# Four output units of an attention stage, moved from steps 6, 7, 9 and 10 to steps 5, 7, 8 and 9

## The chip, the cores and the metric

The kernel runs on one core of one Trainium2 chip. The time is the device time of one execution in microseconds (us). A core has TensorE (PE; PEld is its weight load), VectorE (DVE), ScalarE (ACT), GpSimd (POOL) and SyncE (SP), which issues the weight transfers. The engines run programs of their own and wait for each other through semaphores.

## The reference, cut to what matters

The whole computes two layers with recurrent mixers, then one transformer layer with sliding-window attention and an MLP, for 256 tokens and a width of 1024. The change touches the attention:

```python
def swa_mixer(h, w_qkv, sinks, w_o):
    qkv = h @ w_qkv
    q, k, v = jnp.split(qkv, [SWA_HEADS * HD, (SWA_HEADS + KV) * HD], axis=-1)
    ...
    s = jnp.einsum('bnqkgd,bnskd->bnkgqs', q, kb).astype(jnp.float32) * (HD ** -0.5)
    logits = jnp.where(mask[None, :, None, None], s + bias, NEG)
    m = jnp.maximum(jnp.max(logits, axis=-1, keepdims=True), sink)
    p = jnp.exp(logits - m)
    probs = p / (jnp.sum(p, axis=-1, keepdims=True) + jnp.exp(sink - m))
    o = jnp.einsum('bnkgqs,bnskd->bnqkgd', probs.astype(vb.dtype), vb)
    return o.reshape(B_, T, SWA_HEADS * HD) @ w_o
```

There are 16 heads of 64 columns, 256 tokens in two tiles of 128, and 1024 output columns. The residual, a norm and the MLP follow.

## The kernel before

Matrix products with weights are made of fp32r parts: each operand is split into a high half (a copy rounded to fp32r) and a low half (what is left), and three matmuls are summed (L504 high by high, L505 and L506 the two mixed ones). Weights come in units of 128x1024 in a ring of six slots: SP loads a unit (L436), ACT writes its high half whi (L1132), POOL its low half wlo (L478, L479, raising lo_done), and TensorE raises split_used when it has read one.

**The attention** works on rows r = 0 to 7, each of them two heads. For each row four engines take turns:
- TensorE makes the scores (L1001, L1002) into a pair of PSUM banks. All scores use the same pair, so those of row t wait until VectorE has freed it of row t - 1 (pair_free, a semaphore raised by VectorE's queue at L1620).
- VectorE adds the distance term, takes the minimum (four pieces, L2211), and then makes the reciprocal of the sums of the row before (L2193).
- ScalarE takes the exponentials (four, L1548). GpSimd multiplies by the reciprocals (L463, att_scale).
- TensorE transposes the probabilities (six, L1017), VectorE copies them to pt (L2224, att_pt), and TensorE multiplies them with v (twelve matmuls, L1028 to L1030, att_o).
- ScalarE writes the high half ya_hi of the result (L1555), VectorE the low half ya_lo (L2230, att_ready, one for each row).

The order is written out by hand, in a loop over steps t on each engine. In step t TensorE makes the scores of row t, then a unit of other work if there is one (a q unit for t below 5, an output unit later), then the transposes of row t - 2, then the products with v of row t - 3. ScalarE in step t takes the exponentials of row t and then the high half of row t - 3, which its queue therefore never reaches before the exponentials are done. VectorE in step t reads the scores of row t, then copies the probabilities of row t - 2, then makes the low half of row t - 4; from t = 7 on the low half of row t - 4 comes first.

**The output projection** has two column halves c (512 columns each, one pair of banks each) and four quarters q (two rows each) of the inner dimension. o_unit(c, q) is a whole unit: both tiles of tokens, 12 matmuls of 128x512. It waits for att_ready at 2q + 2, the low halves of rows 2q and 2q + 1, and for q = 0 also for its bank pair (the pair of c = 1 is that of the scores). The units with q of 2 and 3 are cut in halves of one token tile each and follow the loop, as eight half units. In the texts O00, O01, O10 and O11 stand for o_unit(0, 0), (0, 1), (1, 0) and (1, 1); S, T and V with a row's number stand for the scores, the transposes and the products with v of that row.

The lines that place the whole units in the loop on TensorE:

```python
                if t < 5:
                    q_unit((t + 3) // 2, (t + 3) % 2)
                if t in (6, 7, 9, 10):
                    o_unit(t // 9, {6: 0, 7: 1, 9: 0, 10: 1}[t])
                if 2 <= t < 10:
                    r = t - 2
                    pe.wait_ge(att_scale, r + 1)
```

Of the kernel before, what the change touches and what calls it, by code (L numbers as in the profile page):

```python
# [152 lines left out]
def build(nc, a, units, x_turned, p_turned, table, consts, out):  # L153
    with ExitStack() as ctx:
# [247 lines left out]
        def pair_of(name, i):  # L402

            return DB[PAIR[(name, i)]]
# [5 lines left out]
        def score_block(t, head, b):  # L410

            return lg[:, t % 3, LG * head + (P + 1) * b:LG * head + (P + 1) * b + P]
# [80 lines left out]
        def _(pe):  # L493
            at = {"unit": 0}

            def group_start(name, i):

                if BEFORE[(name, i)] > 0:
                    pe.wait_ge(pair_free[PAIR[(name, i)]], BEFORE[(name, i)])
# [30 lines left out]
            def token_unit(name, i, q, xh, xl, start, stop):  # L530

                wh, wl = unit_ready()
                bank = pair_of(name, i)
                for kk in range(SPLK):
                    k = q * SPLK + kk
                    for t in range(NT):
                        tok = slice(t * P, (t + 1) * P)
                        last = three(bank[t][:, :], (xh[:, k, tok], xl[:, k, tok]), (wh[:, kk, :], wl[:, kk, :]),
                                     start=start and kk == 0, stop=stop and kk == SPLK - 1)
                return last  # L540
# [421 lines left out]
            def q_unit(quarter, half):  # L962

                if quarter == 0:
                    bank = pair_of("q_first", 0)[0]
                else:
                    bank = pair_of("q_rest", 0)[(quarter - 1) % 2]
                if half == 0 and quarter < 2:
                    group_start("q_rest" if quarter else "q_first", 0)
                if (quarter, half) == (3, 0):  # L970
                    pe.wait_ge(att_in, 4)
                wide_unit(half, bank, x_hi, x_lo).then_inc(split_used, 1)

            def o_unit(c, q):

                if q == 0:
                    group_start("o_att", c)
                pe.wait_ge(att_ready, 2 * q + 2)
                token_unit("o_att", c, q, ya_hi, ya_lo, q == 0, q == 3).then_inc(split_used, 1)
# [13 lines left out]
            for t in range(11):  # L993
                if t < 8:
                    if t % 2 == 0:
                        pe.wait_ge(att_in, 3 + t // 2)
                    group_start("score", t)
                    bank = pair_of("score", t)
                    for j in range(2):
                        part = slice(j * AD, (j + 1) * AD)  # L1000
                        pe.matmul(bank[j][:, 0:T], qa[part, t, P:T], ka[part, t // 4, :], start=True, stop=True)  # L1001
                        last = pe.matmul(bank[j][:, T:T + P], qa[part, t, 0:P], ka[part, t // 4, 0:P], start=True, stop=True)  # L1002
                    last.then_inc(turned, 1)

                if t < 5:
                    q_unit((t + 3) // 2, (t + 3) % 2)
                if t in (6, 7, 9, 10):
                    o_unit(t // 9, {6: 0, 7: 1, 9: 0, 10: 1}[t])
                if 2 <= t < 10:
                    r = t - 2  # L1010
                    pe.wait_ge(att_scale, r + 1)
                    if r > 0:
                        pe.wait_ge(att_pt, r)
                    for j in range(6):
                        b = high_banks[:, j * P:(j + 1) * P]
                        head, block_ = (j // 2, j % 2) if j < 4 else (j - 4, 2)
                        last = pe.transpose(b, score_block(r, head, block_), ident)  # L1017
                    last.then_inc(att_t, 1)
                if t >= 3:
                    r = t - 3  # L1020
                    pe.wait_ge(att_pt, r + 1)
                    if r - 1 > 0:
                        pe.wait_ge(att_ready, r - 1)
                    v = slice((r // 4) * AD, (r // 4 + 1) * AD)
                    for j in range(2):
                        part = slice(j * AD, (j + 1) * AD)
                        probs = pt[:, r % 2, :]
                        pe.matmul(SB[r % 2][part, 0:P], va[:, 0, v], probs[:, (4 + j) * P:(5 + j) * P], start=True, stop=True)  # L1028
                        pe.matmul(SB[r % 2][part, P:T], va[:, 0, v], probs[:, 2 * j * P:(2 * j + 1) * P], start=True, stop=False)
                        last = pe.matmul(SB[r % 2][part, P:T], va[:, 1, v], probs[:, (2 * j + 1) * P:(2 * j + 2) * P], start=False, stop=True)  # L1030
                    last.then_inc(att_o, 1)
            first = at["unit"]
            at["unit"] += 4
            for t, c, q in ((0, 0, 2), (1, 0, 2), (0, 0, 3), (1, 0, 3), (0, 1, 2), (0, 1, 3), (1, 1, 2), (1, 1, 3)):
# [1429 lines left out]
```

## Time and profile before

| | us |
|---|---|
| median of 3 runs | 918.6 |
| lowest and highest | 918.38 and 918.79 |
| the profiled execution | 918.62 |
| its span in the profile | 916.8 |
| TensorE busy in it | 895.3 |
| POOL, ACT, DVE busy | 674.4, 505.9, 476.2 |

The span is the part of the execution that the profile sees. A row of a timeline gives the start in us from the start of the span, the duration, the engine, the line, the operation, what it writes and reads, shapes, a count where equal ones were merged, and in brackets how long the engine was idle before and what ended it. Matmuls overlap, so a row's end lies behind the start of the next. In the merged rows the duration is that of the whole group. The steps that the change touches lie between 693 and 720 us.

### The profile page before, as it was taken

Reading aid. Unit: us, or ns where it says so; the run is one execution under the profiler, and the core shown is the slowest. Engines: PE = TensorE matmul, PEld = TensorE weight load, DVE = VectorE, ACT = ScalarE, POOL = GpSimd, SP = SyncE. Lnnn points to the kernel's source line nnn. Section 1 sums busy time; section 2 is a strip of 40 time slices with the busy share of each in tenths; the row PEclk is TensorE's granted clock in tenths of the full one; section 3 lists DMA queues with packets and bytes.
Section 4 is the critical chain, followed back from the end, with each engine's and each line's share of the span. In section 5 each row is a group of like instructions: output and inputs, shape, how many; then the busy total and the mean of one; then the engine's idle time right before and its main releaser. Section 6 shows DMA issues by size and latency. Waiting matters only on the chain.

```text
span 916.8 us, 19055 instructions
## 1 busy us (share of the span) xinstructions
PE 895.3 (98%) x7540; PEld 828.6 (90%) x7540; DVE 476.2 (52%) x987; ACT 505.9 (55%) x712; POOL 674.4 (74%) x484
## 2 busy tenths in 40 slices
PE   6999899999999999999999999999999999999997
PEld 6999899998998889999999999888997899998886
DVE  4368865488452533767768777545556442220004
ACT  5775343753336556565677656565566355554431
POOL 5986566566665888967776777769796579889882
PEclk9999999999999999999999999999999999999999
DMA  8663343344443665635444454456552247556631
GB/s 317 203 224 127 127 139 119 120 131 139 140 138 124 209 204 164 207 117 166 157 137 128 153 164 159 138 184 201 179 185 92 93 159 226 190 186 204 205 118 46
DMA packets 41113, 147.14 MB, mean 160 GB/s; under 512 B 4544, under 2 KB 4672, under 8 KB 41024
## 3 DMA queue, kind: packets, MB, share of 16 engines
q1 hardware_dynamic: 39584, 141.76, 47.8%
q10 hardware_dynamic: 1440, 4.16, 1.3%
q8 instruction: 60, 0.98, 0.4%
q14 instruction: 29, 0.24, 0.1%
HBM read 144.86 MB, written 1.05 MB: 159 GB/s over the span
## 4 chain that ended last, share of the span: by engine, by line
PE 89%; DVE 5%; POOL 2%; issue 2%; ACT 2%; DMA 0%; DVEq 0%; ACTq 0%; POOLq 0%
PE dense L504 25%; PE dense L506 24%; PE dense L505 24%; PE bank L872 2%; POOL wlo L479 1%; PE dense L560 1%; POOL wlo L478 1%; PE bank L702 1%; PE bank L703 1%; PE bank L904 1%; PE bank L858 1%; PE bank L1017 1%; PE bank L504 0%; PE bank L506 0%; PE bank L505 0%
## 5 line engine op out<-in xcount | busy, mean ns | idle before, releaser
L479 POOL TENSOR_TENSOR wlo<-raw,whi 128x512 fp32r<-128x512 f32 (+1 forms) x261 | 412.0, 1585 | 25.6 <-ACT whi L1132 25.4
L1132 ACT ACTIVATE whi<-raw 128x1024 fp32r<-128x1024 f32 (+1 forms) x264 | 275.3, 1056 | 226.4 <-PE dense L506 195.8
L478 POOL TENSOR_TENSOR wlo<-raw,whi 128x512 fp32r<-128x512 f32 x197 | 256.4, 1301 | 186.6 <-ACT whi L1132 186.6
L504 PE MATMUL dense<-x_hi,whi 128*128 128x256 f32 x1232 | 353.8, 287 | 8.2 <-DVE wlo L1637 7.3
L505 PE MATMUL dense<-x_lo,whi 128*128 128x256 f32 x1232 | 345.7, 281 | 0.0
L506 PE MATMUL dense<-x_hi,wlo 128*128 128x256 f32 x1232 | 345.7, 281 | 0.0
L504 PEld LDWEIGHTS dense<-x_hi,whi 128*128 128x128 f32 x1232 | 233.9, 190 | 12.1 <-DVE x_lo L1626 7.2
L505 PEld LDWEIGHTS dense<-x_lo,whi 128*128 128x128 f32 x1232 | 235.0, 191 | 0.7 <-issue 0.2
L506 PEld LDWEIGHTS dense<-x_hi,wlo 128*128 128x128 f32 x1232 | 234.5, 190 | 0.0
L504 PE MATMUL dense<-whi,ya_hi 128*128 128x512 f32 x192 | 77.5, 403 | 1.0 <-issue 0.8
L506 PE MATMUL dense<-whi,ya_lo 128*128 128x512 f32 x192 | 75.1, 391 | 0.0
L505 PE MATMUL dense<-wlo,ya_hi 128*128 128x512 f32 x192 | 75.0, 390 | 0.0
L1706 DVE SCALAR_TENSOR_TENSOR cv<-dense,columns,cv 128x255 f32<-128x255 f32 (+2 forms) x72 | 34.7, 481 | 25.8 <-ACT cv L1210 23.2
L504 PEld LDWEIGHTS dense<-whi,ya_hi 128*128 128x128 f32 x192 | 36.1, 188 | 9.0 <-issue 1.7
L506 PEld LDWEIGHTS dense<-whi,ya_lo 128*128 128x128 f32 x192 | 36.1, 188 | 7.8
L505 PEld LDWEIGHTS dense<-wlo,ya_hi 128*128 128x128 f32 x192 | 36.2, 188 | 7.0 <-issue 0.2
L1121 ACT ACT_TABLE_LOAD x32 | 41.1, 1283 | 1.4 <-PEq L2445 0.7
L505 PE MATMUL dense<-wlo,x_hi 128*128 128x256 f32 (+1 forms) x144 | 40.2, 279 | 0.0
L506 PE MATMUL dense<-whi,x_lo 128*128 128x256 f32 (+1 forms) x144 | 40.2, 279 | 0.0
L504 PE MATMUL dense<-whi,x_hi 128*128 128x256 f32 (+1 forms) x144 | 40.1, 278 | 0.0
L2315 DVE TENSOR_TENSOR xtok<-xtok,dense 128x512 f32<-128x512 f32 x2 | 1.4, 686 | 73.6 <-PE dense L506 73.6
L504 PE MATMUL dense<-whi,yb_hi 128*128 128x512 f32 x96 | 37.6, 392 | 0.3 <-POOL wlo L479 0.3
(341 smaller groups left out, 1402.9 us busy)
## 6 DMA issues: line engine op xcount, KB each, us to landing
raw<-weight_units_dram SPq DMA_DIRECT2D x263, 512.0 KB, 3.6
xtok<-in_x_dram SPq DMA_DIRECT2D x1, 1024.0 KB, 7.9
gb<-in_ln_g_dram ACTq DMA_DIRECT2D x2, 512.0 KB, 4.7
gb<-in_ln_b_dram ACTq DMA_DIRECT2D x2, 512.0 KB, 7.0
out_dram<-zt SPq DMA_DIRECT2D x3, 256.0 KB, 2.0
qT<-x_turned_dram SPq DMA_DIRECT2D x2, 256.0 KB, 4.4
raw<-weight_units_dram SPq DMA_DIRECT2D x2, 256.0 KB, 4.9
qT<-x_turned_dram SPq DMA_DIRECT2D x1, 512.0 KB, 7.1
```

Source lines behind the costliest of these rows:

```text
L478: pool.tensor_tensor(wlo[:, slot, 0:half], unit_slot(u)[:, 0:half], whi[:, slot, 0:half].bitcast(F32), ALU.subtract)
L479: pool.tensor_tensor(wlo[:, slot, first:2 * half], unit_slot(u)[:, first:2 * half], whi[:, slot, first:2 * half].bitcast(F32), ALU.subtrac ...
L504: pe.matmul(out_, lh, rh, start=start, stop=False, skip_group_check=True)
L505: pe.matmul(out_, lh, rl_, start=False, stop=False, skip_group_check=True)
L506: return pe.matmul(out_, ll, rh, start=False, stop=stop, skip_group_check=True)
L560: last = pe.transpose(bank[:, j * P:(j + 1) * P], xtok[:, t, k * P:(k + 1) * P], ident)
L702: return pe.matmul(block(SB[2 * g + across], pair, side), block(LT[:, g, :], h, b), block(XN[:, g, :], h, b), start=True, stop=True)
L703: return pe.matmul(SB[2 * g + side][64 * b:64 * b + 64, pair * 32:(pair + 1) * 32], block(EL[:, g, :], 2 * pair + b, side, 256), even_odd( ...
L872: last = pe.matmul(SB[0][rows, u * P:u * P + 96], tokens_of(hk, p % 2, u // 2, u % 2)[:, rows], six, start=True, stop=True)
L1121: act.preload_act_table_set(name)
L1132: act.activation(whi[:, u % NSPL, first:], unit_slot(u)[:, first:], ACT.Copy).then_inc(hi_done, 1)
L1706: link(vec.scalar_tensor_tensor(o, bank[:, i * T:(i + 1) * T - back], colA[:, w:w + 1], o, ALU.mult, ALU.add), conv_done if back == 3 else ...
```

## The change

The first whole unit goes from step 6, between scores and transposes, to the end of step 5, behind the products with v of row 2. The second stays in step 7. The third and the fourth go from steps 9 and 10 to steps 8 and 9, at the same place within the step.

```diff
                 if t < 5:
                     q_unit((t + 3) // 2, (t + 3) % 2)
-                if t in (6, 7, 9, 10):
-                    o_unit(t // 9, {6: 0, 7: 1, 9: 0, 10: 1}[t])
+                if t in (7, 8, 9):
+                    o_unit(t // 8, t % 2)
                 if 2 <= t < 10:
                     r = t - 2
                     pe.wait_ge(att_scale, r + 1)
...
                     last.then_inc(att_o, 1)
+                if t == 5:
+                    o_unit(0, 0)
```

The instructions and their waits stay the same; only TensorE's order differs. The order on TensorE where step 5 passes into step 6, before: the end of V2 (bank01), the scores S6 (dense10, dense11), the beginning of O00 (dense00).

```order
L1028 MATMUL bank01<-pt,va 64x128
L1029 MATMUL bank01<-pt,va 64x128
L1030 MATMUL bank01<-pt,va 64x128
L1001 MATMUL dense10<-ka,qa 128x256 [waits pair_free1,att_in]
L1002 MATMUL dense10<-ka,qa 128x128
L1001 MATMUL dense11<-ka,qa 128x256
L1002 MATMUL dense11<-ka,qa 128x128
L504 MATMUL dense00<-whi,ya_hi 128x512 [waits lo_done,att_ready,pair_free0]
```

And after, at the end of O00, whose twelve matmuls now stand right behind V2: its last rows, S6, and the transposes T4.

```order
L504 MATMUL dense01<-whi,ya_hi 128x512
L505 MATMUL dense01<-wlo,ya_hi 128x512
L506 MATMUL dense01<-whi,ya_lo 128x512
L1001 MATMUL dense10<-ka,qa 128x256 [waits pair_free1,att_in]
L1002 MATMUL dense10<-ka,qa 128x128
L1001 MATMUL dense11<-ka,qa 128x256
L1002 MATMUL dense11<-ka,qa 128x128
L1017 MATMUL bank23<-con,lg 128x128 [waits att_pt,att_scale]
```

The scores of step 6 have moved behind the unit, which keeps its wait for att_ready.

The order on TensorE where step 9 passes into step 10, before: the last matmuls of O11 and the beginning of V7.

```order
L504 MATMUL dense11<-whi,ya_hi 128x512
L505 MATMUL dense11<-wlo,ya_hi 128x512
L506 MATMUL dense11<-whi,ya_lo 128x512
L1028 MATMUL bank01<-pt,va 64x128 [waits att_ready,att_pt]
L1029 MATMUL bank01<-pt,va 64x128
L1030 MATMUL bank01<-pt,va 64x128
```

After: the transposes T7, V6 and V7 in a row.

```order
L1017 MATMUL bank23<-con,lg 128x128 [waits att_pt,att_scale]
L1017 MATMUL bank23<-con,lg 128x128 x5
L1028 MATMUL bank01<-pt,va 64x128 [waits att_ready,att_pt]
L1029 MATMUL bank01<-pt,va 64x128
L1030 MATMUL bank01<-pt,va 64x128
L1028 MATMUL bank01<-pt,va 64x128
L1029 MATMUL bank01<-pt,va 64x128
L1030 MATMUL bank01<-pt,va 64x128
L1028 MATMUL bank01<-pt,va 64x128 [waits att_ready,att_pt]
```

O11 has moved ahead of T7, so between V6 and V7 no unit is left.

## Rows read from the trace of the kernel before

**Rows 1.** The page, part 1: engine, busy us, share of the span, instructions.

```profile
PE 895.3 (98%) x7540; PEld 828.6 (90%) x7540; DVE 476.2 (52%) x987; ACT 505.9 (55%) x712; POOL 674.4 (74%) x484
```

**Rows 2.** List of TensorE's waits, whole span: total us, times, longest.

```profile
PE dense L504 <- DVE wlo L1637: 7.3, 1, 7.3
...
PE dense L504 <- issue: 0.8, 1, 0.8
```

**Rows 3.** Timeline of TensorE, 670 us, then steps 5 to 7.

```profile
670.25 0.71 PE L1001 MATMUL dense<-ka,qa 64*128 64x256 f32 x4
...
671.11 0.38 PE L504 MATMUL dense<-x_hi,whi 128*128 128x256 f32 x1
...
695.26 0.43 PE L1028 MATMUL bank<-pt,va 128*64 128x128 f32 x2
...
697.12 0.71 PE L1001 MATMUL dense<-ka,qa 64*128 64x256 f32 x4 [0.72 <-DVEq L1620]
...
698.86 0.47 PE L504 MATMUL dense<-whi,ya_hi 128*128 128x512 f32 x1 [0.81 <-issue]
...
701.71 0.82 PE L1017 MATMUL bank<-con,lg 128*128 128x128 f32 x6
702.46 0.43 PE L1028 MATMUL bank<-pt,va 128*64 128x128 f32 x2
...
703.53 0.71 PE L1001 MATMUL dense<-ka,qa 64*128 64x256 f32 x4
```

**Rows 4.** Timeline of TensorE, steps 7 to 10.

```profile
704.67 0.50 PE L504 MATMUL dense<-whi,ya_hi 128*128 128x512 f32 x1 [0.20 <-DVE ya_lo L2230]
...
707.53 0.82 PE L1017 MATMUL bank<-con,lg 128*128 128x128 f32 x6
708.27 0.43 PE L1028 MATMUL bank<-pt,va 128*64 128x128 f32 x2
...
709.54 0.85 PE L1017 MATMUL bank<-con,lg 128*128 128x128 f32 x6
...
719.02 0.43 PE L1028 MATMUL bank<-pt,va 128*64 128x128 f32 x2
...
720.10 0.51 PE L504 MATMUL dense<-whi,ya_hi 128*128 128x512 f32 x1
```

**Rows 5.** Timeline of VectorE, steps 5 and 6.

```profile
696.83 0.08 DVE L2211 DVE_READ_ACCUMULATOR2_ANT st_att<- 128x1 f32 x1
...
697.34 0.96 DVE L2224 COPY pt<-bank 128x768 f32<-128x768 f32 x1
698.33 0.42 DVE L2230 TENSOR_TENSOR ya_lo<-bank,ya_hi 128x256 fp32r<-128x256 f32 x1
698.79 0.48 DVE L2211 CUSTOM_DVE_ANT_0 lg<-con,dense,lg 128x256 f32<-128x256 f32 x1
...
700.51 0.08 DVE L2211 DVE_READ_ACCUMULATOR2_ANT st_att<- 128x1 f32 x1
```

**Rows 6.** Timeline of ScalarE, step 6.

```profile
700.66 0.49 ACT L1548 ACTIVATE lg<-lg,st_att 128x257 f32<-128x257 f32 x1
...
702.75 0.19 ACT L1548 ACTIVATION_READ_ACCUMULATOR lg<-lg,st_att 128x1 f32 x1
703.70 0.39 ACT L1555 ACTIVATE ya_hi<-bank 128x256 fp32r<-128x256 f32 x1 [0.77 <-PE bank L1030]
```

**Rows 7.** Timeline of GpSimd: scaling of row 7.

```profile
710.72 1.61 POOL L463 TENSOR_TENSOR lg<-lg,rsum 128x512 f32<-128x512 f32 x2 [2.19 <-DVE rsum L2193]
```

**Rows 8.** TensorE at the start; windows: us, busy (instructions), PEclk (granted clock), DMA, GB/s.

```profile
7.62 0.42 PE L505 MATMUL dense<-x_lo,whi 128*128 128x256 f32 x1
...
13.35 0.29 PE L505 MATMUL dense<-x_lo,whi 128*128 128x256 f32 x1
...
910.00:914.00 4.00, 0.82 (x7) 0.62 (x6) 2.85 (x8) 1.13 (x3) 1.45 (x2) 1.00 0.00 0
914.00:915.00 1.00, 0.00 (x0) 0.00 (x0) 0.00 (x0) 0.00 (x0) 0.00 (x0) 0.72 0.45 172
```

## The prediction

> **What bounds the kernel now.** I read the page's first part, then the list of waits, then the timelines of the attention stage engine by engine. TensorE is busy for 895.3 of 916.8 us [rows 1], so a change of order can move the time only where TensorE stands still. The list of its waits has eight lines for the whole span; the longest, 7.3 us, is the start of the kernel, and one of 0.8 us is the wait ahead of the first output unit, which the change moves [rows 2]. The list names no wait of TensorE from 705 us to its last matmul, so what is lost in the attention stage is handed on to the end whole, with nothing behind it that takes it up. Of the matmuls nothing is added or removed, so the question is one sum: how long TensorE waits in steps 5 to 10 before, and how long after.
>
> The timeline before [rows 3, 4], in starts. The products with v of row 2 (V2, step 5) start at 695.26. Such a group holds the queue for 1.07 us (702.46 to 703.53), so TensorE could go on at 696.33. The scores of step 6 (S6) start at 697.12: **0.79 us** of wait, for the bank pair, which VectorE frees after it has read the scores of step 5 (last piece 696.83 to 696.91, 0.21 us before S6 starts) [rows 3, 5]. S6 takes 0.86 us (670.25 to 671.11, a group of scores that nothing held up), which gives 697.98; unit O00 (column half 0, quarter 0) starts at 698.86: **0.88 us**. Scores S7 start at 703.53, so could end the slot at 704.39; unit O01 starts at 704.67: **0.28 us**. The products V4 end their slot at 709.34 and the transposes T6 start at 709.54: **0.20 us**. Together TensorE waits 2.15 us. From T6 on, the rows join without a hole up to the first half unit at 720.10.
>
> What O00 waits for: it needs att_ready at 2, which is the low half of row 1, a subtraction on VectorE at 698.33 of 0.42 us. It ends at 698.75, and O00 starts 0.11 us later [rows 3, 5]. The row's releaser reads "issue", not VectorE, which leaves a doubt; see rival B. VectorE comes to that subtraction after the scores of step 5 and the copy of the probabilities (697.34, 0.96 us). None of these waits for anything that the change moves, so 698.75 stays.
>
> **The change part by part.** 48 matmuls of 128x512 (four units of 12) change places. A unit is 2.86 us in the queue wherever it stands (704.67 to 707.53), the transposes 0.75 (701.71 to 702.46) [rows 3, 4]. No DMA is issued from TensorE's queue. I now lay out the changed order with these durations.
>
> Step 5. O00 stands right behind V2, ahead of S6. TensorE is free at 696.33, the operand comes at 698.75, so O00 starts at 698.86 as before: a wait of **2.53 us**. S6, which filled part of this before, now stands behind the waiting unit and starts at 701.71 instead of 697.12, 4.6 us later. That is the point of the whole sum, since S6 is what three other engines live on.
>
> Step 6. T4 at 702.57, V3 at 703.32, free at 704.39. VectorE reads S6 when its last matmul ends, 0.94 us from its start, so from 702.75 instead of 698.79; the four pieces take 1.80 us (698.79 to 700.59) [rows 5] and end at 704.55. S7 needs the pair freed, 0.21 us later: 704.76, a wait of **0.37 us** where there was none.
>
> Step 7. S7 to 705.62. O01 needs att_ready at 4, the low half of row 3. Its high half is written by ScalarE, and in ScalarE's order that stands behind the four exponentials of step 6. These took from 700.66 to 702.94 [rows 6] and now start behind VectorE's pieces, at 704.61, and end at 706.89. The high half (0.39 us) ends at 707.31, VectorE's subtraction (0.42 us) runs 707.41 to 707.83, O01 starts at 707.90: a wait of **2.28 us** instead of 0.28. Before, this high half waited for V3 alone (703.70, after ScalarE had stood idle for 0.77 us) [rows 6], since the exponentials were long done.
>
> Steps 7 to 10. T5 at 710.76, V4 711.51, O10 712.58 (its pair is free once VectorE has read S7, 707.87 to 709.67), T6 715.44, V5 716.19, O11 717.26, T7 720.12, V6 720.87, free at 721.94. The wait ahead of T6 is gone (0.20 us), because O10 stands over the copy that it waited for. At the end the reverse happens: no unit stands between V6 and V7 any more. V7 needs the copy of T7's transposes: T7's last matmul ends 0.84 us from its start, 720.96, the copy runs 721.05 to 722.01, and V7 starts at 722.13: a wait of **0.19 us**. The first half unit follows 1.08 us later (719.02 to 720.10) [rows 4], at 723.21 instead of 720.10.
>
> The sum: waits 2.53 + 0.37 + 2.28 + 0.19 = 5.37 against 2.15 us, +3.22; by the starts, 723.21 - 720.10 = +3.11, since the slots differ by a few hundredths. I take **+3.1 us**. The profiled execution took 918.62 us, the median is 918.6, so both lead to 921.7.
>
> What I cost at nothing, and its cover. GpSimd scales row 5 from about 705.0 to 706.6 (1.61 us) [rows 7], 4 us before T5 needs it; row 6 and row 7 likewise end 3 us and more ahead. The split of the seventh weight unit of the projection follows the scaling of row 7, which ends about 715.5; its first reader is the fifth half unit, at 723.21 plus four times 1.43 (half of 2.86), about 729, 13 us later. The low half of row 7 ends 1.0 us after V7 as before and is read 2.8 us after the first half unit. Nothing there comes near.
>
> **The clock.** Over 910 to 914 us the granted clock is 1.00 although the last matmul ends at 910.82; in the next microsecond it is 0.72 [rows 8]. So 3.2 us of idle did not take the 2.4 GHz level away in this trace, and the two new holes are 2.5 and 2.3 us. At the start of the kernel, after 7.3 us of idle [rows 2], matmuls of 128x256 ran at 0.42 us each, and from 13.35 at 0.29 [rows 8], the 1.2 GHz and the 2.4 GHz level. The Trainium skill (TensorE: Matmul & The Clock Gate, "HAM oscillation — how this bites in real kernels") speaks against this change in general: long pauses between groups of matmuls let the chip halve the array's clock, and the work after each pause then starts slow. By that rule the sum would be rival C's, by the rows here it is the +3.1 above.
>
> **The rivals.**
> A, the forecast: both waits as laid out, 921.7 us. Its own range: without the two small waits (0.37 and 0.19) +2.5, less the 0.4 us spread of the runs, 920.7; with 0.1 us more at each of the eight handovers, 922.5.
> B, not slower: O00 does not wait for the low half of row 1. The row at 698.86 names "issue" as its releaser, while that at 704.67 names VectorE; if the 0.88 us belong to S6 itself or the sequencer, O00 starts at 696.33 in its new place. Then S6 is at 699.2, VectorE ends it at 702.1, S7 waits 0.37 us (702.24), exponentials end at 704.4, and O01 starts at 705.4; with the same steps behind it the first half unit comes at 720.7, +0.6: 919.2 us. It decides from the point at which O00 starts before about 697.6, which would bring the sum under 1.84 us. Against it: the semaphore's raise and the start are 0.11 us apart. Even then nothing is gained, since S6's delay alone eats the 0.88 us.
> C, slower still: one hole brings the 1.2 GHz level. At the start the low level held from 7.3 to 13.3 us, for 6 us of matmuls [rows 2, 8], half of it lost: at most +3.0 us for one hole, 924.7; for both 927.7. Against it: the clock row at the end.
> D, faster: all waits of steps 5 to 10 vanish, -2.15 us at most, 916.5. It needs the operand of O00 2.5 us earlier, for which nothing in VectorE's order moves.
> That the change does not take place is excluded, as the order of the built kernel shows it.
>
> **How the numbers follow.** A 0.82, B 0.08, C 0.07, D 0.03. A measurement of this kernel can tell about 0.2%, 1.84 us, from no change. Slower by more is A but for its lower edge and C: 0.87; within: B and that edge, 0.10; faster: 0.03. The range is A's, opened upward to most of one hole of C: 920.7 to 924.4.
>
> **What the profile after would show.** O00's first matmul at 698.9 with 2.4 us idle ahead, ending what was S6's place; S6 at 701.7; ScalarE's first exponential of step 6 near 704.6; O01 near 707.9 with over 2 us idle ahead and VectorE's ya_lo as releaser; a small hole ahead of V7; no hole ahead of T6; the first half unit near 723.2; the granted clock 1.00 throughout; every stage behind shifted by 3.1 us. The prediction is wrong if O00 starts at 696.4 (B), if units after a hole take over 4 us (C), or if a hole of over 0.5 us opens or closes anywhere behind 724 us.

## The result and the profile after

| | us |
|---|---|
| before, median of 6 runs | 918.69 (918.38 to 918.97) |
| after, median of 6 runs | 924.25 (921.95 to 925.72) |
| ratio, with its 95% interval | 1.0059 (1.0048 to 1.0069) |
| the profiled execution after, and its span | 924.71 and 922.8 |

The changed kernel is slower by 5.6 us. The range on record holds the time by 0.15 us; the forecast point, 921.7, was 2.5 us too low, so little more than half of the loss was foreseen. The runs after also spread over 3.8 us, those before over 0.6 us. Two lines of the list of waits answer to the one shown in [rows 2] (total in us, times, longest):

```profile
PE dense L504 <- issue: 2.5, 1, 2.5
PE dense L504 <- DVE ya_lo L2232: 2.3, 1, 2.3
```

The hole ahead of O00 is 2.5 us and that ahead of O01 2.3 us, as laid out. From O01's start to the end of the span the list names no further wait of TensorE. The page's first line against [rows 1]:

```profile
PE 897.8 (97%) x7540; PEld 829.6 (90%) x7540; DVE 476.8 (52%) x987; ACT 505.8 (55%) x712; POOL 673.9 (73%) x484
```

TensorE is busy 2.5 us longer, although its matmuls are the same 7540. So holes alone are not the whole loss. The timeline of TensorE, against [rows 3, 4]:

```profile
695.03 0.43 PE L1028 MATMUL bank<-pt,va 128*64 128x128 f32 x2
...
698.63 0.53 PE L504 MATMUL dense<-whi,ya_hi 128*128 128x512 f32 x1 [2.46 <-issue]
...
700.24 0.63 PE L505 MATMUL dense<-wlo,ya_hi 128*128 128x512 f32 x1
...
703.14 0.71 PE L1001 MATMUL dense<-ka,qa 64*128 64x256 f32 x4
...
704.80 0.43 PE L1028 MATMUL bank<-pt,va 128*64 128x128 f32 x2
...
706.13 0.71 PE L1001 MATMUL dense<-ka,qa 64*128 64x256 f32 x4 [0.18 <-DVEq L1622]
...
709.34 0.79 PE L504 MATMUL dense<-whi,ya_hi 128*128 128x512 f32 x1 [2.28 <-DVE ya_lo L2232]
...
713.70 0.82 PE L1017 MATMUL bank<-con,lg 128*128 128x128 f32 x6
...
725.03 0.43 PE L1028 MATMUL bank<-pt,va 128*64 128x128 f32 x2
...
726.10 0.50 PE L504 MATMUL dense<-whi,ya_hi 128*128 128x512 f32 x1
```

In starts: V2 at 695.03, O00 at 698.63, S6 at 703.14. The unit O00 takes 4.51 us where a unit took 2.86; eight of its twelve matmuls take about 0.6 us instead of 0.39. S7 at 706.13 to O01 at 709.34, and O01 takes 4.36 us. The other groups keep their slots, but for the short waits ahead of S7 and V7. The windows of the same kernel (span, busy us and instructions of the five engines, then PEclk, the granted clock, with 1.00 for full speed, then DMA) say why:

```profile
697.00:699.00 2.00, 0.37 (x2) 0.34 (x3) 1.46 (x3) 1.90 (x8) 1.98 (x3) 0.98 0.31 51
699.00:702.00 3.00, 3.00 (x9) 2.32 (x8) 0.00 (x0) 1.46 (x3) 1.41 (x2) 0.50 0.35 141
702.00:703.00 1.00, 1.00 (x5) 0.65 (x3) 0.00 (x0) 0.00 (x0) 1.00 (x1) 0.84 0.00 0
703.00:709.00 6.00, 3.88 (x35) 2.96 (x34) 3.39 (x12) 2.58 (x9) 1.73 (x3) 1.00 0.28 87
709.00:710.00 1.00, 0.66 (x2) 0.56 (x3) 0.93 (x4) 0.00 (x0) 0.00 (x0) 0.57 0.00 0
710.00:712.00 2.00, 2.00 (x6) 1.58 (x5) 1.23 (x7) 0.75 (x3) 0.41 (x1) 0.50 0.00 0
712.00:713.00 1.00, 1.00 (x5) 0.74 (x4) 0.00 (x0) 0.95 (x4) 1.00 (x2) 0.72 0.00 0
...
740.00:905.00 165.00, 165.00 (x1098) 152.02 (x1098) 29.22 (x46) 82.22 (x95) 144.86 (x61) 1.00 0.57 179
```

The granted clock is 0.50 from about 698.9 to 702.3 and again from about 709.1 to 712.6, that is the 1.2 GHz level, once behind each hole. Before, the stage ran at 1.00 throughout. From 740 to 905 us TensorE is busy without a gap at 1.00, as it was before, and from the first half unit to the end of the span both kernels take 196.7 us (916.8 - 720.10 and 922.8 - 726.10), so nothing behind the stage takes anything up.

The account of the profiled executions, from the start of V2 to the first half unit: 24.84 us before (695.26 to 720.10), 31.07 after (695.03 to 726.10), +6.2. Of this the waits (ahead of O00, S7, O01 and V7) are 2.53 + 0.26 + 2.35 + 0.11 = 5.25 against 2.15, **+3.1**, and the two slow units 1.65 + 1.50, **+3.1**.

The chain to O01 is seen on VectorE and ScalarE, against [rows 5, 6]:

```profile
698.11 0.42 DVE L2232 TENSOR_TENSOR ya_lo<-bank,ya_hi 128x256 fp32r<-128x256 f32 x1
704.22 0.48 DVE L2213 CUSTOM_DVE_ANT_0 lg<-con,dense,lg 128x256 f32<-128x256 f32 x1 [5.69 <-PE dense L1002]
...
705.93 0.08 DVE L2213 DVE_READ_ACCUMULATOR2_ANT st_att<- 128x1 f32 x1
...
708.86 0.42 DVE L2232 TENSOR_TENSOR ya_lo<-bank,ya_hi 128x256 fp32r<-128x256 f32 x1 [1.00 <-ACT ya_hi L1557]
```

```profile
706.05 0.51 ACT L1550 ACTIVATE lg<-lg,st_att 128x257 f32<-128x257 f32 x1 [5.54 <-DVE st_att L2213]
...
708.16 0.19 ACT L1550 ACTIVATION_READ_ACCUMULATOR lg<-lg,st_att 128x1 f32 x1
708.38 0.38 ACT L1557 ACTIVATE ya_hi<-bank 128x256 fp32r<-128x256 f32 x1
```

VectorE has nothing to do for 5.7 us until S6 exists, reads it from 704.22 to 706.01, the exponentials of ScalarE run from 706.05 to 708.35, the high half of row 3 ends at 708.76, and the low half that O01 waits for ends at 709.28. Each link is within 0.1 us of its length in the prediction; all of it lies 1.4 us later than forecast, because the slow first unit took 1.65 us more and V2 had started 0.23 us earlier.

### The profile page after: what moved, and what is told of

It reads as the page before. It is cut to its first block, busy times and chain, and to the rows that moved or that the text cites. A ratio compares the mean times of both kernels' runs of the same rounds, so it can differ in the third digit from the quotient of the medians.

```text
span 922.8 us, 19055 instructions
## 1 busy us (share of the span) xinstructions
PE 897.8 (97%) x7540; PEld 829.6 (90%) x7540; DVE 476.8 (52%) x987; ACT 505.8 (55%) x712; POOL 673.9 (73%) x484
## 4 chain that ended last, share of the span: by engine, by line
PE 85%; DVE 6%; ACT 3%; issue 2%; POOL 2%; DMA 0%; DVEq 0%; ACTq 0%; POOLq 0%
PE dense L504 24%; PE dense L505 23%; PE dense L506 23%; PE bank L872 2%; POOL wlo L479 1%; DVE cv L1708 1%; POOL wlo L478 1%; PE dense L560 1%; PE bank L702 1%; ACT whi L1134 1%; PE bank L703 1%; PE bank L904 1%; PE bank L858 1%; PE bank L504 0%; PE bank L505 0%
```

## The experiments

The theory behind them: two costs of about equal size, the time TensorE waits and the lower clock that follows a wait; both come from moving O00 ahead of the scores of step 6. The names of the kernels are those of the runs. The kernel before was measured again beside each of three groups: 918.82 us (16 runs, 917.79 to 919.91) with only_first, only_later, fill_first and fill_both; 918.61 (29 runs, up to 921.07) with low1_early, hi3_early, both_early and before_low1; 918.56 (13 runs) with fill_second and low1_fill. Each ratio is against before in its own group.

### Which move costs: only_first and only_later

only_first moves O00 alone:

```diff
-                if t in (6, 7, 9, 10):
-                    o_unit(t // 9, {6: 0, 7: 1, 9: 0, 10: 1}[t])
+                if t in (7, 9, 10):
+                    o_unit(t // 9, {7: 1, 9: 0, 10: 1}[t])
...
+                if t == 5:
+                    o_unit(0, 0)
```

> The order before, with O00 alone moved to the end of step 5 (O10 and O11 stay in steps 9 and 10). Theory: all of the loss comes from this one move, since it delays the scores of step 6 by 4.6 us, which opens a hole ahead of O00 (2.5 us) and one ahead of O01 (2.3 us), and the granted clock falls to 0.50 behind both: 924 to 925 us, like the changed kernel, with 0.2 us of wait ahead of T6 and none ahead of V7. Rival: the moves of O10 and O11 carry part of it (V6 and V7 without a unit between them, later copies): 921 to 922.5 us.

Measured: 924.41 us (four runs, 924.19 to 924.68), ratio 1.0061 (1.0046 to 1.0076). The list of waits:

```profile
PE dense L504 <- issue: 2.4, 1, 2.4
PE dense L504 <- DVE ya_lo L2232: 2.3, 1, 2.3
```

And the windows, with the two stretches at the low clock:

```profile
699.00:703.00 4.00, 4.00 (x14) 2.87 (x12) 0.00 (x0) 1.33 (x2) 2.52 (x2) 0.61 0.24 97
...
709.00:712.00 3.00, 2.82 (x7) 2.27 (x8) 1.99 (x10) 0.92 (x3) 0.57 (x1) 0.50 0.00 0
```

The one move has the whole loss, with the same two holes and the same two falls.

only_later moves the other two units and leaves O00:

```diff
-                if t in (6, 7, 9, 10):
-                    o_unit(t // 9, {6: 0, 7: 1, 9: 0, 10: 1}[t])
+                if t in (6, 7, 8, 9):
+                    o_unit(t // 8, t % 2)
```

> The order before, with O10 and O11 alone moved to steps 8 and 9 (O00 stays in step 6). Theory: no change that can be measured, 918.6 us within 0.3: the 0.2 us wait ahead of T6 goes and 0.2 us ahead of V7 comes. Rival (these moves carry part of the loss): 920 us or more. No stretch with a granted clock under 1.00 between 690 and 725 us by either.

Measured: 918.71 us (ten runs, 917.78 to 919.31), ratio 0.9999 (0.999 to 1.0009). These moves cost nothing that can be measured.

### Waits apart from clock: fill_first, fill_both, fill_second

A hole is filled with matmuls on ready operands, whose results nobody reads. They end at about the moment at which the awaited operand is there, so that the unit starts where it did and only TensorE's activity in the wait changes. fill_first has the 18 ahead of O00 alone, fill_second the 14 ahead of O01 alone, fill_both has both:

```diff
+            def filler(n, bank):
+                for _ in range(n):
+                    pe.matmul(bank[:, 0:T], x_hi[:, 0, 0:P], x_hi[:, 0, :], start=True, stop=True)
...
                 if t in (7, 8, 9):
+                    if t == 7:
+                        pe.wait_ge(att_pt, 5)
+                        filler(14, SB[2])
                     o_unit(t // 8, t % 2)
...
                 if t == 5:
+                    group_start("o_att", 0)
+                    filler(18, pair_of("o_att", 0)[0])
                     o_unit(0, 0)
```

> The changed kernel with 18 matmuls of 128x256 on ready operands between V2 and O00, into the bank that O00 then starts anew; they take about 2.1 us, less than the hole of 2.46 us. Theory (waits and clock are two separate costs, 3.1 us each in the profiled run): O00 still starts 0.1 us after the low half of row 1, but at the granted clock of 1.00, so the unit takes 2.9 instead of 4.5 us; the second hole and its fall of the clock stay: 923.1 us. Rival (the slow units are a result of the wait itself, not of what TensorE did in it): 924.3 us, as without the matmuls. Second rival (the fall behind the second hole needs the first one, since little was done between): 921.7 us.

Measured: 923.91 us, but from 921.35 to 925.45 over five runs, ratio 1.005 (1.0033 to 1.0066). The profiled execution is the longest of these; in its timeline O00, S6 and O01:

```profile
699.74 0.47 PE L504 MATMUL dense<-whi,ya_hi 128*128 128x512 f32 x1
...
702.65 0.71 PE L1006 MATMUL dense<-ka,qa 64*128 64x256 f32 x4
...
708.86 0.80 PE L504 MATMUL dense<-whi,ya_hi 128*128 128x512 f32 x1 [2.28 <-DVE ya_lo L2239]
```

```profile
699.00:703.00 4.00, 3.88 (x22) 2.93 (x22) 0.60 (x2) 2.51 (x7) 2.40 (x4) 1.00 0.41 131
709.00:714.00 5.00, 5.00 (x12) 3.93 (x13) 1.70 (x9) 2.20 (x8) 1.61 (x2) 0.50 0.00 0
```

The filled hole is followed by a unit of 2.91 us (699.74 to 702.65) at a clock of 1.00. The second hole, left as it was, is followed by a fall, and here the clock stays down for 6.8 us, from about 708.2 to 715.0, over the unit and all that follows it up to there. So the first rival falls: it is what TensorE does in the wait, and not the wait, that decides. The second rival, that no fall comes behind the second hole, held, by the time and the mean clock, in one run of five (921.35 us, 0.997). The median lay 0.8 us above my 923.1. One fall can cost more than the 1.5 us that I had taken: in this profile V2 to the first half unit took 30.83 us, 2.89 more than with both holes filled (below). Whether that is what raised the median is not shown, since the other runs have no trace.

> As fill_first, and 14 more such matmuls between S7 and O01, into a free bank, behind the copy of the probabilities of row 4; about 1.7 us in a hole of 2.3 us. Theory: the clock stays at 1.00 throughout and the two waits are left alone, which gives the predicted sum, 921.7 us, with little spread between runs. Rival (the waits cost more than 3.1 us by themselves): 923 us or more.

Measured: 921.49 us, 921.25 to 921.98 over six runs, ratio 1.0029 (1.0017 to 1.0041). The timeline, with V2, the first filling (L977), O00, S7, the second filling, O01 and the first half unit:

```profile
694.80 0.43 PE L1036 MATMUL bank<-pt,va 128*64 128x128 f32 x2
...
695.87 2.41 PE L977 MATMUL dense<-x_hi 128*128 128x256 f32 x18
698.38 0.47 PE L504 MATMUL dense<-whi,ya_hi 128*128 128x512 f32 x1
...
704.29 0.71 PE L1006 MATMUL dense<-ka,qa 64*128 64x256 f32 x4 [0.19 <-DVEq L1632]
...
705.62 1.94 PE L977 MATMUL bank<-x_hi 128*128 128x256 f32 x14 [0.40 <-DVE pt L2236]
707.50 0.50 PE L504 MATMUL dense<-whi,ya_hi 128*128 128x512 f32 x1
...
722.74 0.50 PE L504 MATMUL dense<-whi,ya_hi 128*128 128x512 f32 x1
```

```profile
694.00:723.00 29.00, 28.29 (x199) 23.16 (x200) 13.47 (x40) 12.06 (x33) 13.91 (x14) 1.00 0.22 70
```

V2 to O00 is 3.58 us (3.60 in the kernel after), S7 to O01 3.21 us (3.21): the units start when they did, only the clock is held. VectorE has the two operands ready at 698.28 and 707.44, and the filling ends at 698.28 and 707.56 (the end of a matmul lies behind the start of the next), so it takes up the wait to its end and delays neither unit visibly. From V2 to the first half unit it is 27.94 us, 3.10 more than before. This is the forecast +3.11 measured by itself; the medians of the group differ by 2.7 us (921.49 - 918.82), which the interval of the ratio, 1.6 to 3.8 us, does not tell from it.

> The changed kernel with the 14 matmuls in the second hole alone. It completes the table of holes filled and left: none filled 924.3, the first 923.9 (with runs from 921.4 to 925.5), both 921.5 us. Theory (each fall of the clock costs about 1.5 us, and each hole brings its own): the first hole's fall stays, the second's goes: 923.1 us, granted clock 0.50 for about 3 us from 699 us and 1.00 from 706. Rival (the second fall alone makes the price, since the first hole is met by a low clock that other work would absorb): 921.7 us.

Measured: 923.47 us (four runs, 923.0 to 923.64), ratio 1.0051 (1.0036 to 1.0066). The windows:

```profile
700.00:703.00 3.00, 3.00 (x9) 2.32 (x8) 0.00 (x0) 0.96 (x1) 1.96 (x2) 0.50 0.21 86
704.00:710.00 6.00, 5.42 (x49) 4.50 (x46) 3.90 (x13) 2.58 (x9) 1.62 (x2) 1.00 0.27 87
```

The fall behind the first hole stays, the second is gone, and nothing absorbs the first: in the profile V2 to the first half unit takes 29.59 us, 1.65 above fill_both, and the median lies 2.0 us above it. The first hole was followed by a fall in every profile in which it was left open (after, only_first, fill_second, hi3_early), but one run of the changed kernel, 921.95 us at a mean clock of 0.996, lies where fill_both does and so had none, as far as time and mean clock can tell.

| medians, us | second hole open | second hole filled |
|---|---|---|
| first hole open | 924.25 | 923.47 |
| first hole filled | 923.91 | 921.49 |

Three groups of runs meet in this table, whose medians of before lie between 918.56 and 918.82 us.

### What the holes wait for: low1_early, hi3_early, both_early

low1_early lets VectorE make the low half of row 1 first in step 5:

```diff
-                if t >= 7:
+                if t >= 7 or t == 5:
                     att_low(t - 4)
...
-                if 4 <= t < 7:
+                if t in (4, 6):
                     att_low(t - 4)
```

> The changed kernel, with VectorE making the low half of row 1 at the start of step 5, ahead of its reading of the scores, and not at its end. Theory (O00 waits for that low half alone, and both of its results, the hole and the slow unit, go with the wait): O00 starts at about 696.4 with no hole and runs at a granted clock of 1.00; S6 at 699.2; the second hole, ahead of O01, stays at 2.3 us, since the high half of row 3 still stands behind the exponentials of step 6, and the clock may fall behind it: 919.2 us without that fall, 920.7 with it. Rival (the releaser named as issue was another wait, or S6's delay by itself costs the rest): O00 stays at 698.6 and the time at 923 to 924.5 us.

Measured: 919.67 us over ten runs, 918.83 to 923.05, ratio 1.0012 (1.0001 to 1.0022). V2, O00, S7 and O01 in the timeline:

```profile
695.73 0.43 PE L1028 MATMUL bank<-pt,va 128*64 128x128 f32 x2
...
696.80 0.50 PE L504 MATMUL dense<-whi,ya_hi 128*128 128x512 f32 x1
...
702.74 0.71 PE L1001 MATMUL dense<-ka,qa 64*128 64x256 f32 x4 [0.18 <-DVEq L1622]
...
705.95 0.50 PE L504 MATMUL dense<-whi,ya_hi 128*128 128x512 f32 x1 [2.28 <-DVE ya_lo L2232]
```

```profile
690.00:730.00 40.00, 37.40 (x254) 30.51 (x254) 19.86 (x56) 19.12 (x48) 25.25 (x22) 1.00 0.26 85
```

O00 follows V2 without a hole, 1.07 us after its start, which settles what the releaser "issue" of [rows 3] stood for: the low half of row 1, and nothing else. The hole ahead of O01 is 2.28 us as forecast, and in this profile no fall comes behind it: the clock is 1.00 from 690 to 730 us. Eight of the ten runs lie between 918.8 and 920.5 us with a mean clock of 0.995 or 0.996, the other two at 920.8 and 923.1 with 0.992 and 0.994; no trace shows where their clock fell.

hi3_early lets ScalarE write the high half of row 3 ahead of the exponentials of step 6:

```diff
+                if t == 6:
+                    act.wait_ge(att_o, t - 2)
+                    act.activation(ya_hi[:, t - 3, :], SB[(t - 3) % 2][:, 0:T], ACT.Copy).then_inc(att_hi, 1)
+                    settle(att_hi)
                 if t < 8:
                     act.wait_ge(att_neg, t + 1)
...
-                if t >= 3:
+                if t >= 3 and t != 6:
                     act.wait_ge(att_o, t - 2)
```

> The changed kernel, with ScalarE writing the high half of row 3 ahead of the exponentials of step 6, not behind them. Theory (the second hole is the chain S6, VectorE's reading, exponentials, high half, low half): O01 starts 1.0 us earlier with respect to S7, a wait of 1.3 instead of 2.3 us, and with so short a hole the clock behind it stays at 1.00; the first hole and its fall stay: 922.2 us. Rival (O01 waits for VectorE's own queue, not for ScalarE): the hole stays at 2.3 us and the time at 924 us.

Measured: 922.72 us, four runs from 921.51 to 924.45, so a loose figure, ratio 1.0043 (1.0026 to 1.0059). The list of waits:

```profile
PE dense L504 <- issue: 2.4, 1, 2.4
PE dense L504 <- DVE ya_lo L2236: 1.3, 1, 1.3
```

The wait ahead of O01 is 1.3 instead of 2.3 us. The exponentials in front of the high half were 1.0 us of it. Behind so short a hole the profile shows no fall, as expected.

> The changed kernel with both: the low half of row 1 first in VectorE's step 5, the high half of row 3 first in ScalarE's step 6. Theory: no hole over 1.3 us, the granted clock 1.00 throughout, and the two long waits replaced by the wait for the bank pair and 1.3 us ahead of O01: 918.3 us, the same as the kernel before within 0.2%. Rival (moving the scores of step 6 behind the unit has a price of its own on GpSimd or in the weight ring, that these waits hide): 920 us or more.

Measured: 918.41 us (917.85 to 919.92, eleven runs), ratio 0.9997 (0.9988 to 1.0005). The stage at a granted clock of 1.00 throughout:

```profile
690.00:730.00 40.00, 38.36 (x259) 31.34 (x258) 20.75 (x58) 19.42 (x48) 25.27 (x22) 1.00 0.28 91
```

With both operands made earlier, the moved order costs nothing and gains nothing that can be measured. Here S6 comes only 2.2 us later behind V2 than before. That scores delayed in full have no other price is shown by fill_both, where the waits make up all of the 3.10 us.

### The spread, and a version of before: low1_fill and before_low1

low1_fill is low1_early with the 14 matmuls in the hole ahead of O01.

> low1_early (the low half of row 1 first in VectorE's step 5) with the 14 matmuls in its one hole ahead of O01. Theory (two of ten runs of low1_early, at 920.8 and 923.1 us with a granted clock of 0.992 and 0.994, lay high by a fall of the clock behind that hole, so filling it takes these away and leaves the rest): median 919.3 us, no run above 921. Rival (the spread has nothing to do with that hole): the same spread, with one run in five above 920.7.

Measured: 918.95 us, ten runs from 918.63 to 920.26, ratio 1.0004 (0.9994 to 1.0013), none above 921. That agrees with the theory but does not show it: two high runs in ten are few, and the kernel before reached 921.07 us once in 29 runs.

before_low1 is the kernel before with the edit of low1_early.

> The kernel before, with the low half of row 1 first in VectorE's step 5. Theory: the wait of 0.88 us ahead of O00 goes, the one ahead of S6 grows by the 0.45 us that VectorE now spends earlier, so about 0.4 us are won: 918.3 us, less than can be told from no change. Rival (each wait of TensorE in the stage counts in full, 0.9 us won): 917.8 us.

Measured: 918.18 us (917.13 to 920.19, twelve runs), ratio 0.9995 (0.9986 to 1.0005). The waits in its profile:

```profile
PE dense L1001 <- DVEq L1620: 1.0, 1, 1.0
...
PE dense L504 <- DVE ya_lo L2230: 0.3, 1, 0.3
```

The 0.8 us ahead of O00 is gone from the list, the one ahead of S6 has grown from 0.7 to 1.0. The median is 0.4 us lower, as worked out, but the interval holds 1: no version was found that is clearly faster than before.

## Why the prediction was right, and where it was not

**The range.** That it held 924.25 is in good part luck. Forecast A, with 0.82 of the chance, ended at 922.5; the range reached to 924.4 only because it was opened towards rival C, which had 0.07, and it is C's sign that came: "units after a hole take over 4 us". They took 4.51 and 4.36. The median is about the sum of A's waits and two falls of the clock at half of C's price each (921.7 + 2 x 1.5 = 924.7), and no line of the prediction has that sum.

**What bounds the kernel, and that nothing is absorbed behind.** Right. The windows from 740 to 905 us, the equal 196.7 us behind the first half unit, and the account that closes within the stage show it.

**O00 keeps its start, S6 goes behind it.** Right: a wait of 2.53 us by the starts, forecast 2.53. The doubt of rival B was settled by low1_early, against B. B's own estimate, 919.2 us for O00 starting at once, is what low1_early made of it by other means (919.67).

**The second hole through VectorE, ScalarE and VectorE.** Right: 2.35 against 2.28 us. hi3_early took out one link of the chain and the hole shrank by that link.

**The small waits.** S7 0.26 against 0.37, V7 0.11 against 0.19, T6's gone. Right in sign, about 0.1 us too large. That O10 and O11 cost nothing was right, by only_later.

**The sum of the waits.** +3.11 forecast, +3.10 in fill_both, where the waits stood alone.

**The clock.** This is the step that failed. I gave 0.07 to rival C and took the clock as 1.00 in the likeliest case, because 3.2 us of idle at the end of the kernel had not yet lowered it [rows 8] while the new holes were 2.5 and 2.3 us. That compared lengths of single pauses, and one pause that the level survived is no bound from which a shorter one is safe. After, the level fell 2.7 us after the last matmul ahead of the first hole (about 696.2 to 698.9) and 2.1 us after the last one ahead of the second (707.1 to 709.1), against 3.6 us at the end of the kernel before (910.8 to 914.4). Over all profiles with a fall in the stage this time runs from 1.6 us (second hole of fill_first) to 3.9 us (first hole of hi3_early, where the level fell 1.5 us after O00 had started).

The trace of the kernel before had the counterexample, and I had not looked there. Near 96 us, TensorE stands still for 1.87 us, makes 16 small matmuls, and stands still for 0.77 us more; from about 98.6 to 102.0 us its granted clock is 0.50:

```profile
96.48 0.68 PE L765 MATMUL bank<-XN,LT 64*64 64x64 f32 x16 [1.87 <-DVE VB L1771]
...
99.00:102.00 3.00, 3.00 (x16) 3.00 (x15) 2.79 (x7) 0.65 (x2) 3.00 (x4) 0.50 0.21 42
```

All twelve profiles of this case show a fall there, in eight of them already before the second of the two pauses is over (in fill_second from 95.7 us, when the matmuls behind the first pause, 95.25 to 96.03, were still running). So the first, of 1.9 us, can be enough. Two of them (both_early and fill_first) have another at about 213 us, behind a wait of 1.4 or 1.0 us and one of 0.8 us. So it could be read from this trace that pauses shorter than the new holes can be followed by a fall, and rival C deserved much more than 0.07. These other falls also move the times and mean clocks of whole runs, so where a single run is read by these alone, as below, it is an indication only.

The same holes did not always bring a fall: the first one brought none in one run of six of the changed kernel, the second one brought one in four runs of five of fill_first and in one or two of ten of low1_early, by the time and the mean clock. What the Trainium skill says in general (TensorE: Matmul & The Clock Gate, "HAM oscillation — how this bites in real kernels"), that pauses between groups of matmuls let the chip halve the array's clock and that the work behind starts slow, agrees with the trace, which has a clock of 0.50 behind each hole. But the pauses of which it warns are longer than these 2.46 and 2.28 us, so by its figure neither would have brought a fall; here the measurement decides. The same page says ("What's actually happening") that the point of the switch is not tied to the kernel's start and so varies from run to run; within one group of runs the spread was 4.1 us with the second hole open (fill_first) and 0.7 us with both filled, which agrees. The runs of before in that group spread by 2.1 us themselves, so the spread alone is weak evidence.

**Its size.** Rival C's price for one fall was at most 3.0 us, from the start of the kernel. The granted clock of the profile says 1.00 there, from 8 to 13 us; only the pace of the matmuls speaks for the low level, 0.213 us for 256 columns against 0.427 for 512 in the stretches at 0.50. In the profile after each fall cost 1.5 to 1.65 us, in that of fill_first 2.9. Between medians the first one costs 2.0 us if the second hole is filled (923.47 - 921.49) and the second 2.4 us if the first is (923.91 - 921.49), but both together 2.8 us (924.25 - 921.49), so with both open probably not every run has two full falls.

What remains open: why the second hole of fill_first was followed by a fall more often than the equally long one of low1_early, which lies about 3 us earlier, and why the low level lasts 3.4 us in some falls and twice that in others (6.8 us in fill_first, and near 96 us in six of the twelve profiles). No run here separates these.

## What to carry to other kernels

Work that is put in front of a waiting engine must not stand in front of the instruction that feeds the other engines: O00 waited the same time as before, but the scores behind it were what VectorE, ScalarE and, through them, the next unit lived on, so one wait became two. Where a change opens a pause of some 2 us on TensorE, count the pause and a following stretch at half clock as a case of its own with real weight, and not as a remote one. Look through the whole trace of the kernel before for pauses of like length and the granted clock behind them; one place that looks safe is not enough. To separate the two costs, fill the pause with matmuls that nobody reads.

## What the runs showed of the hardware

- Two pauses of 2.3 to 2.5 us, with 8.4 us between them (698.63 to 707.06), each brought the granted clock from 1.00 to 0.50 in the profile after; 128x512 matmuls then took 0.63 us instead of 0.39. In the profile of low1_early a pause of 2.28 us brought no fall, and pauses of 1.31 us brought none in those of hi3_early and both_early.
- A pause of about 1.9 us and one of 0.4 to 0.8 us shortly behind it, near 96 us, came with a fall in all twelve profiles, in eight of them before the second pause was over; the level was low for 3.4 us in six of them and for 6.8 us in the other six.
- The level came back after 3.4 us, twice, in the profile after, and after 6.8 us in that of fill_first, with TensorE busy for all but at most the first 0.7 us.
- 18 and 14 matmuls of 128x256 on data that was lying ready held the level through the same pauses in the profile of fill_both and cost nothing that shows: 3.10 us over the stage before, against 3.10 from the waits of the profile after.
